# Attention units of 512 queries instead of 256 in a float32 decoder trunk

## The chip, the cores and the metric

The kernel runs on one core of one Trainium2 chip, in one launch. The metric is device time in microseconds (us); lower is better. The engines are named as in the profile: PE is the matrix engine, PEld its weight loads, DVE the vector engine, ACT the scalar engine, POOL the GpSimd engine, SP the engine that only issues DMAs. PE writes its products into PSUM, which holds 8 banks of 512 float32 per partition; four tiles `ps0` to `ps3` of two banks each cover it.

## The reference

One batch of 1024 tokens of width 1024 goes through two layers. The first layer mixes tokens with a gated linear recurrence (RG-LRU), the second with attention over 16 heads of width 64, with a forget gate; each is followed by a SwiGLU feed-forward of width 2816. All is float32. The change touches the attention of the second layer alone:

```python
for blk in range(S // Q_BLOCK):                 # 8 blocks of 128 queries
    q0, q1 = blk * Q_BLOCK, (blk + 1) * Q_BLOCK
    s = einsum('bhqd,bhkd->bhqk', q[:, :, q0:q1], k[:, :, :q1]) * HEAD_DIM ** -0.5
    s = s + c[:, :, q0:q1, None] - c[:, :, None, :q1]   # c: running sum of log forget gates
    s = where(mask, s, -inf)                    # causal
    p = softmax(s, axis=-1)
    outs.append(einsum('bhqk,bhkd->bhqd', p, v[:, :, :q1]))
```

## The kernel before, in words

Every float32 product is built from parts: an operand is split into a high part (float32r, ACT writes it) and a low part (the rest, DVE subtracts it), and PE multiplies high by high, high by low and low by high. The recurrent layer and its feed-forward take the first 990 us, the attention runs from about 1004 to 1494 us, and its output product and the second feed-forward fill the rest.

The attention goes through 8 pairs of heads, `pair(i, uses, with_p)`. Each of PE, ACT and DVE runs its own version of that function, and all three walk through the same list of steps (`pair_steps`), each doing its share of a step and skipping steps in which it has none. So the list sets the program order of all three engines at once. Each engine executes its instructions in that order; an instruction that waits for a semaphore holds back all that stand behind it on its engine. Before the change a pair has 8 units: 2 heads times 4 ranges of 256 queries, in the order 3, 0, 2, 1 (`RANGE_ORDER`). The steps are:

- `S0`, `S1`: the scores of one block of 128 queries of the **next** unit against all its keys. PE multiplies (`scores`), DVE applies the causal mask and finds the row's maximum in place in PSUM (one long instruction and a short one that reads the accumulator), ACT writes the exponentials to `probs` (`exponentials`), again with a short accumulator read, and then the tile is free ("drained"). Score tiles alternate between `ps0` and `ps1`.
- `T0`, `T1`, ...: PE transposes blocks of 128x128 exponentials of this unit into one bank of `ps2` (the two banks take turns), ACT copies the bank to `pth` (high part), DVE subtracts to `ptl` (low part). The first T of a unit waits for the exponentials of the unit's last blocks; every T waits for the `ptl` of the T two before.
- `V0`, `V1`, ...: PE multiplies the values `vs` of a block of keys by `pth` and `ptl` of the T of that number and adds up in `o_ps`, a part of `ps3`. It waits for that `ptl`.
- `O`: the finished unit is taken out of `o_ps`: ACT copies 64 partitions to `o_low`, DVE adds them to the other 64 and writes `resid`. V0 of the next unit waits for it.
- `p`: one eighth of a half of the next pair's K and Q projection, three matmuls of 512 columns. These depend on nothing of this pair, and fill PE while ACT and DVE work. Every eighth p, DVE takes the half out of PSUM. The last pair has 28 parts of the output projection in their place.
- `A`, `B` at the start: the two halves of the V projection, 24 matmuls each; `X` turns the result by 8 transposes, ACT copies it (high part of `vs`, two instructions) and `Y` is DVE's two subtractions (low part). V0 of unit 0 waits for Y. `R` turns the row sums.

Tables hang further ACT and DVE work of 1024 columns on named steps: `HI_AT` and `LO_AT` the split of the next weights, `HIGH_O_AT` and `LOW_O_AT` (last pair) the split of the attention output. After V0 of the last unit ACT also runs `high_k`, four copies of the next pair's K (lines 2119 and 2124). `tiles.plan` and `Turns` count the uses of each PSUM tile, so that waits can name them.

The lines that matter below: PE L1440 projection, L1452 and L1453 scores, L1472 transposes, L1485 values, L1518 X; ACT L2162 exponentials, L2187 and L2188 X, L2197 the copy to `pth`, L2202 `o_low`; DVE L3100 the V projection's drain, L3105 and L3106 Y, L3114 mask and maximum, L3121 `ptl`, L3130 O.

Of the kernel before, what the change touches and what calls it, by code (L numbers as in the profile page):

```python
# [11 lines left out]
P = 128  # L12
# [37 lines left out]
class FeedForward:  # L50
# [8 lines left out]
    def first_part(self, n, half):  # L59
# [10 lines left out]
RANGE_ORDER = [3, 0, 2, 1]  # L70
UNIT_STEPS = [
# [19 lines left out]
]  # L91
PAIR_START = "A S0 S1 B"
FIRST_START = "A B S0 S1"
# [11 lines left out]
FIRST_LO_AT = {(-1, "B"): "K", (3, "V0"): "Q", (6, "T2"): "nextV"}  # L105
# [7 lines left out]
def pair_steps(with_p, first):  # L113

    steps = [(-1, s) for s in (FIRST_START if first else PAIR_START).split()]
    units = UNIT_STEPS if with_p else LAST_UNIT_STEPS
    for u, unit in enumerate([FIRST_UNIT] + units[1:] if first else units):
        steps += [(u, s) for s in unit.split()]
    steps.append((len(UNIT_STEPS), "O"))
    return steps  # L120


def hawk_fox_yoco(nc, x, norm_mix, norm_ffn, w_ffn_in, w_ffn_out, w_rec_in, conv_w, conv_b,
# [21 lines left out]
    RANGES = QB // 2  # L145
# [25 lines left out]
    tiles.plan("att", [1, 0, 1] + [0, 1] * (UNITS - 1) + [0], PAIRS).plan("attE", [1, 2, 0, 1, 2, 0, 1, 2, 2])  # L171
# [25 lines left out]
    with ExitStack() as life:  # L197
# [85 lines left out]
        with ExitStack() as att:  # L283
# [17 lines left out]
            probs = [sb(f"probs{b}", [P, 2, S // (b + 1)], F32, att) for b in range(2)]  # L301
# [4 lines left out]
            o_low = [sb(f"o_low{b}", [HD, 2 * P], F32, att) for b in range(2)]  # L306
# [48 lines left out]
        o_ps = ps[3][:, 0:2 * P]  # L355
# [545 lines left out]
        def _(pool):  # L901
# [38 lines left out]
            def pool_pair(i, uses, next_k=None):  # L940
                pool.wait_ge(ql_ready, i * 2 + 2)
                pool.wait_ge(o_added, i * UNITS + 1)
# [3 lines left out]
                pool.wait_ge(o_added, i * UNITS + 4)  # L946
# [86 lines left out]
        def _(pe):  # L1033
# [422 lines left out]
            def blocks_of(r, m):  # L1456

                if m < r:
                    return [(2 * m, 0, 0), (2 * m + 1, 0, 2 * P)]
                return [(2 * m, 0, 0), (2 * m + 1, 1, 2 * P)]  # L1460

            def transposes(i, u, m):
                t = tiles_before(u) + m
                if m == 0:
                    for half in range(2):
                        slot, n = s_tile(i, u, half)
                        pe.wait_ge(drained[slot], n)
                if t >= 2 or not (isinstance(i, int) and i == 0):
                    pe.wait_ge(ptl_ready, i * T_PAIR + (t - 1))
                for kb, q0, col in blocks_of(range_of(u), m):  # L1470
                    for q in range(q0, 2):
                        last = pe.transpose(t_ps[t % 2][:, col + (q - q0) * P:col + (q - q0 + 1) * P],  # L1472
                                            probs[u % 2][:, q, kb * P:(kb + 1) * P], ident[:, :])
                last.then_inc(t_filled, 1)

            def values(i, u, m):
# [19 lines left out]
            def pair(i, uses, with_p=True):  # L1496
# [3 lines left out]
                for u, step in pair_steps(with_p, is_first(i)):  # L1500
                    m = int(step[1]) if len(step) > 1 else 0
                    if step in "AB":
                        half = "AB".index(step)
# [4 lines left out]
                        elif is_first(i):  # L1508
                            pe.wait_ge(f_drained, 2)
                        for k in range(KT):  # L1510
                            projection_part(f_bank(step), uses["V"], half, k, v_filled)
                        f += 1
                        f_read = f_before(i) + f
# [1735 lines left out]
```

## Time and profile before

| | |
|---|---|
| time, median of 3 runs | 2226.4 us (2226.28 to 2227.3) |
| span of the profiled execution, first to last instruction | 2225.0 us |
| PE busy | 2200.1 us, 99% of the span |
| DVE busy | 1674.3 us, 75% |
| ACT busy | 1181.8 us, 53% |
| POOL busy | 360.3 us, 16% |
| one pair of heads, from the same step to the same step | 60.65 us |

The profiled execution shows its span alone; what lies around it is taken as the 1.4 us that the median is longer. PE's matmuls are pipelined: a row's duration (0.39 us for 512 columns) runs into the next one's, and the time that an instruction costs PE is the distance from its start to the next start (0.23 us). The same holds in smaller measure for ACT and DVE. A short wait of PE can hide in that overlap.

### The profile page before, as it was taken

The numbers are of one execution on the slowest core, as the hardware profiler recorded it, in microseconds if no ns is written. First come the engines' busy times: TensorE is split into PE (matmuls) and PEld (weight loads), VectorE is DVE, ScalarE is ACT, GpSimd is POOL, SyncE is SP. The second block draws the span as 40 slices with busy tenths as digits, with TensorE's granted clock in tenths as the row PEclk, the third lists the DMA queues.
The fourth block names the chain that finished last, engine by engine and source line by source line (L and its number), as shares of the span: only waits on it lengthen the run. The fifth ranks groups of instructions, "written<-read, shape, count | busy, mean of one in ns | idle before, by whom it ended". The sixth has DMA issues, their size and how long they took to land.

```text
span 2225.0 us, 28679 instructions
## 1 busy us (share of the span) xinstructions
PE 2200.1 (99%) x10393; PEld 1832.6 (82%) x10393; DVE 1674.3 (75%) x2353; ACT 1181.8 (53%) x1873; POOL 360.3 (16%) x352
## 2 busy tenths in 40 slices
PE   8999999999999999999999999999999999999998
PEld 7888887888888888887888888888888888888886
DVE  7677788787778777688666766775777778888866
ACT  5543576355555555356666666754535555555525
POOL 4000000022222222021111111102002222222200
PEclk9999999999999999999999999999999999999999
DMA  5120300367676676431111111132136666666652
GB/s 152 48 59 26 95 15 24 133 133 133 132 133 133 127 131 124 129 115 29 39 30 39 39 39 39 30 105 76 39 133 117 126 124 128 127 129 128 129 168 86
DMA packets 208983, 208.03 MB, mean 93 GB/s; under 512 B 9704, under 2 KB 153296, under 8 KB 208848
## 3 DMA queue, kind: packets, MB, share of 16 engines
q0 software_dynamic: 39168, 75.51, 20.7%
q1 hardware_dynamic: 167952, 126.43, 19.1%
q10 hardware_dynamic: 1728, 4.31, 0.7%
q8 instruction: 81, 1.33, 0.2%
q14 instruction: 54, 0.44, 0.1%
HBM read 122.28 MB, written 83.95 MB: 93 GB/s over the span
## 4 chain that ended last, share of the span: by engine, by line
PE 93%; DVE 4%; ACT 1%; issue 1%; DMA 0%; ACTq 0%; POOL 0%; DVEq 0%; POOLq 0%
PE ps L1239 37%; PE ps L1044 18%; PE ps L1327 14%; PE ps L1440 10%; PE ps L1485 3%; PE ps L1472 3%; PE ps L1576 3%; PE ps L1453 1%; PE ps L1452 1%; PE ps L1555 1%; PE ps L1129 0%; PE ps L1518 0%; PE ps L1093 0%; PE ps L1412 0%; PE ps L1395 0%
## 5 line engine op out<-in xcount | busy, mean ns | idle before, releaser
L972 POOL DMA_DIRECT2D spill<-c x256 | 223.6, 926 | 727.1 <-DVE c L2698 498.4
L2567 DVE TENSOR_TENSOR ring_l<-raw_ffn,ring_h 128x512 fp32r<-128x512 f32 x320 | 222.4, 697 | 154.6 <-ACT ring_h L1804 153.2
L1804 ACT ACTIVATE ring_h<-raw_ffn 128x512 fp32r<-128x512 f32 x320 | 198.8, 625 | 196.5 <-PE ps L1239 103.7
L1897 ACT ACTIVATE c<-ps 128x512 f32<-128x512 f32 x256 | 150.2, 597 | 13.2
L1440 PE MATMUL ps<-xh,wh_att 128*128 128x512 f32 x368 | 148.6, 404 | 1.6 <-DVE wl_att L2269 1.6
L2162 ACT ACTIVATE probs<-ps,nmax 128x896 f32<-128x896 f32 (+7 forms) x128 | 95.1, 743 | 99.0 <-DVE nmax L3114 97.2
L1804 ACT ACTIVATE ring_h<-w_sum 128x512 fp32r<-128x512 f32 x112 | 69.5, 624 | 147.2 <-PE ps L1044 38.9
L1440 PE MATMUL ps<-xh,wl_att 128*128 128x512 f32 x368 | 143.9, 391 | 0.0
L1440 PE MATMUL ps<-xl,wh_att 128*128 128x512 f32 x368 | 143.9, 391 | 0.0
L3121 DVE TENSOR_TENSOR ptl<-ps,pth 128x512 fp32r<-128x512 f32 (+1 forms) x160 | 96.8, 634 | 51.8 <-ACT pth L2197 50.5
L2698 DVE TENSOR_TENSOR c<-ps,c 128x512 f32<-128x512 f32 x192 | 123.4, 683 | 4.8 <-PE ps L1327 4.5
L2306 DVE TENSOR_TENSOR resid<-ps,resid 128x1024 f32<-128x1024 f32 x76 | 92.3, 1220 | 39.3 <-PE ps L1044 31.6
L2197 ACT ACTIVATE pth<-ps 128x512 fp32r<-128x512 f32 (+1 forms) x160 | 82.8, 553 | 35.0 <-PE ps L1472 25.0
L1327 PE MATMUL ps<-hl,ring_h 128*128 128x512 f32 x256 | 99.8, 390 | 0.0
L1327 PE MATMUL ps<-hh,ring_h 128*128 128x512 f32 x256 | 99.7, 390 | 0.0
L1327 PE MATMUL ps<-hh,ring_l 128*128 128x512 f32 x256 | 99.6, 389 | 0.0
L3114 DVE CUSTOM_DVE_ANT_0 ps<-ps,causal 128x896 f32<-128x896 f32 (+7 forms) x128 | 94.5, 774 | 0.0
L2567 DVE TENSOR_TENSOR ring_l<-w_sum,ring_h 128x512 fp32r<-128x512 f32 x112 | 76.5, 684 | 22.0 <-ACT ring_h L1804 22.0
L1472 PE MATMUL ps<-ident,probs 128*128 128x128 f32 x576 | 81.5, 275 | 2.1 <-DVE ptl L3121 1.2
L1440 PEld LDWEIGHTS ps<-xh,wl_att 128*128 128x128 f32 x368 | 69.1, 188 | 15.6
L1485 PE MATMUL ps<-pth,vs 128*128 128x256 f32 x320 | 80.6, 279 | 0.7 <-DVE ptl L3121 0.4
L1440 PEld LDWEIGHTS ps<-xh,wh_att 128*128 128x128 f32 x368 | 69.3, 188 | 12.8 <-issue 2.0
(411 smaller groups left out, 6305.5 us busy)
## 6 DMA issues: line engine op xcount, KB each, us to landing
spill<-c POOLq DMA_DIRECT2D x256, 256.0 KB, 5.9
raw_ffn<-in_w_ffn_in SPq DMA_DIRECT2D x88, 512.0 KB, 5.3
raw_ffn<-in_w_ffn_out SPq DMA_DIRECT2D x44, 512.0 KB, 7.3
resid<-spill SPq DMA_DIRECT2D x24, 512.0 KB, 7.2
raw<-in_w_rec_in SPq DMA_DIRECT2D x16, 512.0 KB, 5.6
spill<-resid POOLq DMA_DIRECT2D x16, 512.0 KB, 3.0
raw_att<-in_w_kvf SPq DMA_DIRECT2D x16, 512.0 KB, 4.0
xin<-in_x SPq DMA_DIRECT2D x4, 1024.0 KB, 9.8
```

Source lines behind the costliest of these rows:

```text
L972: pool.dma_start(spill[m, :, half * BANK:(half + 1) * BANK], block[:, :], accum_op=ALU.add).then_inc(sem, 16)
L1044: last = pe.matmul(acc[:, h], w, v[:, h], start=(first and p == 0), stop=(final and p == 2))
L1239: last = pe.matmul(acc, w, v, start=(start and k == 0 and p == 0), stop=(k == 3 and p == 2), skip_group_check=True)
L1327: last = pe.matmul(acc, a, v, start=(i in (P1, P2, P5) and p == 0), stop=(p == 2), skip_group_check=True)
L1440: last = pe.matmul(acc, w, v[:, k, h], start=(k == 0 and p == 0), stop=(k == KT - 1 and p == 2))
L1472: last = pe.transpose(t_ps[t % 2][:, col + (q - q0) * P:col + (q - q0 + 1) * P], probs[u % 2][:, q, kb * P:(kb + 1) * P], ident[:, :])
L1485: last = pe.matmul(o_ps[:, q0 * P:2 * P], v, pt[t % 2][:, col:col + n], start=(kb == 0 and pt is pth), stop=(kb == 2 * r + 1 and pt is ptl))
L1804: act.activation(F.ring_h[slot][:, :], src, ACT.Copy).then_inc(F.unit_hi, 1)
L1897: act.activation(dst[:, :], y if what == "s5" else w, ACT.Copy).then_inc(out_tapped, 1)
L2567: dve.tensor_tensor(F.ring_l[slot][:, :], src, F.ring_h[slot][:, :].bitcast(F32), ALU.subtract).then_inc(F.unit_lo, 1)
L2698: dve.tensor_tensor(c, w if what == "C22" else y, c, ALU.add).then_inc(out_joined, 1)
L3121: dve.tensor_tensor(ptl[t % 2][:, 0:width], t_ps[t % 2][:, 0:width], pth[t % 2][:, 0:width].bitcast(F32), ALU.subtract).then_inc(ptl_ready, 1)
```

## The change

A unit now is one head and 512 queries, so a pair has 4 units: for each head first the wide range (queries 512 to 1023, against up to 1024 keys), then the narrow one (queries 0 to 511). Each unit has four score blocks S0 to S3 of the next unit. A T tile holds one block of keys against up to four blocks of queries, in place of two blocks of keys against two blocks of queries; the last three key blocks of the diagonal are packed as 384 + 128 and 256 columns. A wide unit has 7 T tiles and a narrow one 3, so a pair has 20 as before. The V matmuls have up to 512 columns, `o_ps` grows from 256 to 512 columns, and `o_low` with it. The V projection is cut as A, B, C, with B and C four eighths each of the second half. The score tiles keep alternating between `ps0` and `ps1`. All step strings and the tables that hang work on steps are new.

```diff
-RANGE_ORDER = [3, 0, 2, 1]
+RANGE_ORDER = [1, 0]
 UNIT_STEPS = [
-    "T0 T1 X p p Y S0 T2 T3 p V0 V1 S1 p p V2 V3",
-    "O T0 S0 S1 p V0 p p",
...
-    "O T0 T1 R p p p p V0 V1",
+    "T0 X T1 p p p Y V0 T2 p V1 T3 S0 p V2 T4 S1 p V3 T5 S2 p V4 T6 S3 p V5 V6",
+    "O T0 T1 S0 S1 p p V0 T2 p p S2 S3 V1 p p V2 p p",
+    "O T0 T1 p p V0 T2 p V1 T3 S0 p V2 T4 S1 p V3 T5 S2 p V4 T6 S3 p V5 p V6",
+    "O T0 T1 p p V0 T2 R p p V1 p p V2 p p",
 ]
+FIRST_UNIT = "p X Y p T0 T1 p p V0 T2 p V1 T3 S0 p V2 T4 S1 p V3 T5 S2 p V4 T6 S3 p V5 V6"
+FIRST_THIRD = "O T0 T1 p V0 T2 p V1 T3 S0 p V2 T4 S1 p V3 T5 S2 p V4 T6 S3 p V5 V6"
+FIRST_FOURTH = "O T0 T1 p p V0 T2 R p V1 p V2 p p"
 LAST_UNIT_STEPS = [
+    "T0 X T1 Y V0 T2 p V1 T3 S0 p V2 T4 S1 V3 T5 S2 p V4 T6 S3 p V5 V6",
+    "O T0 T1 S0 S1 p p V0 T2 p p S2 S3 V1 p p V2 p p",
...
-PAIR_START = "A S0 S1 B"
-FIRST_START = "A B S0 S1"
+PAIR_START = "A S0 S1 B S2 S3 C"
+FIRST_START = "A B C S0 S1 p p p S2 S3"
...
-HI_AT = {(-1, "A"): "K", (3, "T1"): "Q", (4, "V2"): "nextV"}
-LO_AT = {(-1, "S1"): "K", (3, "V0"): "Q", (6, "T2"): "nextV"}
+HI_AT = {(-1, "A"): "K", (1, "V0"): "Q", (2, "V2"): "nextV"}
+LO_AT = {(-1, "S1"): "K", (1, "V1"): "Q", (3, "T2"): "nextV"}
...
-            o_low = [sb(f"o_low{b}", [HD, 2 * P], F32, att) for b in range(2)]
+            o_low = [sb(f"o_low{b}", [HD, BANK], F32, att) for b in range(2)]
...
-        o_ps = ps[3][:, 0:2 * P]
+        o_ps = ps[3][:, 0:BANK]
...
             def blocks_of(r, m):
-                if m < r:
-                    return [(2 * m, 0, 0), (2 * m + 1, 0, 2 * P)]
-                return [(2 * m, 0, 0), (2 * m + 1, 1, 2 * P)]
+                if m <= 4 * r:
+                    return [(m, 0, 0)]
+                if m == 4 * r + 1:
+                    return [(m, 1, 0), (m + 2, 3, 3 * P)]
+                return [(m, 2, 0)]
...
             def transposes(i, u, m):
                 if m == 0:
-                    for half in range(2):
-                        slot, n = s_tile(i, u, half)
-                        pe.wait_ge(drained[slot], n)
+                    for n in range(2, 4):
+                        slot, count = s_tile(i, u, n)
+                        pe.wait_ge(drained[slot], count)
```

ACT's program in the first unit of a pair, before (a pair in the loop, from X to the unit's end; `pth<-ps` is the copy of a T, `probs` the exponentials of an S, `vs` is X):

```order
L2187 ACTIVATE vs<-ps 128x8x64
L2188 ACTIVATE vs<-ps 128x8x64
L2162 ACTIVATE probs,rsum<-ps,nmax 128x128
L2197 ACTIVATE pth<-ps 128x512
L2197 ACTIVATE pth<-ps 128x384
L2162 ACTIVATE probs,rsum<-ps,nmax 128x256
L2202 ACTIVATE o_low<-ps 64x256
```

The same place in the changed kernel:

```order
L2171 ACTIVATE probs,rsum<-ps,nmax 128x1024
L2206 ACTIVATE pth<-ps 128x512
L2196 ACTIVATE vs<-ps 128x8x64
L2197 ACTIVATE vs<-ps 128x8x64
L2206 ACTIVATE pth<-ps 128x512 x3
L2171 ACTIVATE probs,rsum<-ps,nmax 128x128
L2206 ACTIVATE pth<-ps 128x512
L2171 ACTIVATE probs,rsum<-ps,nmax 128x256
L2206 ACTIVATE pth<-ps 128x512
L2171 ACTIVATE probs,rsum<-ps,nmax 128x384
L2206 ACTIVATE pth<-ps 128x256
L2171 ACTIVATE probs,rsum<-ps,nmax 128x512
```

Before, two copies and two exponentials follow X; now the copy of T1 stands behind X, and four exponentials alternate with copies, one each, down to the unit's end.

ACT's program at the end of a pair, before (`kh` are the four copies of `high_k`, `o_low` the step O):

```order
L2202 ACTIVATE o_low<-ps 64x256
L2197 ACTIVATE pth<-ps 128x512
L2197 ACTIVATE pth<-ps 128x384
L2119 ACTIVATE kh<-kv_tmp 64x1024 x2
L2124 ACTIVATE kh<-kh 64x1024 x2
L2219 DMA rinv_dram<-rinv_rows 16x128
L2202 ACTIVATE o_low<-ps 64x256
```

And in the changed kernel:

```order
L2211 ACTIVATE o_low<-ps 64x512
L2206 ACTIVATE pth<-ps 128x512 x2
L2128 ACTIVATE kh<-kv_tmp 64x1024 x2
L2133 ACTIVATE kh<-kh 64x1024 x2
L2206 ACTIVATE pth<-ps 128x256
L2228 DMA rinv_dram<-rinv_rows 16x128
L2211 ACTIVATE o_low<-ps 64x512
```

The four copies of K stood behind the last T of the pair; now the copy of the last T, T2, stands behind them.

## Rows read from the trace of the kernel before

**Rows 1.** The page's busy shares, and the engines of its chain.
```profile
PE 2200.1 (99%) x10393; PEld 1832.6 (82%) x10393; DVE 1674.3 (75%) x2353; ACT 1181.8 (53%) x1873; POOL 360.3 (16%) x352
PE 93%; DVE 4%; ACT 1%; issue 1%; DMA 0%; ACTq 0%; POOL 0%; DVEq 0%; POOLq 0%
```

**Rows 2.** One pair of heads in the view by stretches, with its columns.
```profile
core 0: us, PE busy (x) PEld busy (x) DVE busy (x) ACT busy (x) POOL busy (x), PEclk, DMA share, GB/s
1258.47:1319.13 60.66, 60.58 (x355) 52.54 (x354) 41.38 (x77) 38.55 (x73) 10.12 (x6) 1.00 0.13 36
```

**Rows 3.** Timeline of PE, unit 0 and 1 (start, duration, instruction, count).
```profile
1264.86 1.06 PE L1518 MATMUL ps<-ident,kv_tmp 128*128 128x128 f32 x8
1265.68 0.48 PE L1440 MATMUL ps<-xh,wh_att 128*128 128x512 f32 x1
1266.00 0.39 PE L1440 MATMUL ps<-xl,wh_att 128*128 128x512 f32 x1
1266.23 0.40 PE L1440 MATMUL ps<-xh,wl_att 128*128 128x512 f32 x1
...
1268.83 0.28 PE L1485 MATMUL ps<-pth,vs 128*128 128x256 f32 x1
1268.94 0.28 PE L1485 MATMUL ps<-ptl,vs 128*128 128x256 f32 x1
...
1272.11 0.22 PE L1485 MATMUL ps<-pth,vs 128*128 128x128 f32 x1
1272.17 0.28 PE L1485 MATMUL ps<-ptl,vs 128*128 128x128 f32 x1
1272.44 0.52 PE L1472 MATMUL ps<-ident,probs 128*128 128x128 f32 x3
```

**Rows 4.** Timeline of DVE, units 0 and 2; in brackets idle time and its releaser.
```profile
1264.02 0.69 DVE L3100 TENSOR_TENSOR kv_tmp<-ps,rstd 128x512 f32<-128x512 f32 x1 [1.79 <-PE ps L1440]
...
1267.69 0.68 DVE L3106 TENSOR_TENSOR vs<-ps,vs 128x512 fp32r<-128x512 f32 x1
1268.29 0.29 DVE L3114 CUSTOM_DVE_ANT_0 ps<-ps,causal 128x128 f32<-128x128 f32 x1
...
1270.18 1.15 DVE L3121 TENSOR_TENSOR ptl<-ps,pth 128x512 fp32r<-128x512 f32 x2 [1.55 <-ACT pth L2197]
1271.26 0.42 DVE L3114 CUSTOM_DVE_ANT_0 ps<-ps,causal 128x256 f32<-128x256 f32 x1
...
1279.42 0.56 DVE L3114 CUSTOM_DVE_ANT_0 ps<-ps,causal 128x384 f32<-128x384 f32 x1
...
1279.89 0.73 DVE L3114 CUSTOM_DVE_ANT_0 ps<-ps,causal 128x512 f32<-128x512 f32 x1
1280.54 0.14 DVE L3114 DVE_READ_ACCUMULATOR2_ANT nmax<- 128x1 f32 x1
```

**Rows 5.** Timeline of ACT, the same stretches, and the end of the pair.
```profile
1266.45 0.59 ACT L2188 ACTIVATE vs<-ps 128x512 fp32r<-128x512 f32 x1
1268.67 0.37 ACT L2162 ACTIVATE probs<-ps,nmax 128x128 f32<-128x128 f32 x1 [1.62 <-DVE nmax L3114]
...
1269.55 0.98 ACT L2197 ACTIVATE pth<-ps 128x512 fp32r<-128x512 f32 x2 [0.43 <-PE ps L1485]
1271.77 0.47 ACT L2162 ACTIVATE probs<-ps,nmax 128x256 f32<-128x256 f32 x1 [1.24 <-DVE nmax L3114]
...
1280.06 0.58 ACT L2162 ACTIVATE probs<-ps,nmax 128x384 f32<-128x384 f32 x1 [1.40 <-DVE nmax L3114]
...
1280.71 0.69 ACT L2162 ACTIVATE probs<-ps,nmax 128x512 f32<-128x512 f32 x1
...
1281.39 0.48 ACT L2197 ACTIVATE pth<-ps 128x384 fp32r<-128x384 f32 x1
...
1308.70 2.12 ACT L2119 ACTIVATE kh<-kv_tmp 64x1024 fp32r<-64x1024 f32 x2
```

**Rows 6.** The last 5 us of the span in the view by stretches, columns as in rows 2.
```profile
2220.00:2225.00 5.00, 0.00 (x0) 0.00 (x0) 2.11 (x4) 0.53 (x3) 0.00 (x0) 0.51 0.57 219
```

More of the change, by code:

```diff
@@ L116, in pair_steps @@
     units = UNIT_STEPS if with_p else LAST_UNIT_STEPS
-    for u, unit in enumerate([FIRST_UNIT] + units[1:] if first else units):
+    for u, unit in enumerate([FIRST_UNIT, units[1], FIRST_THIRD, FIRST_FOURTH] if first else units):
         steps += [(u, s) for s in unit.split()]
@@ L184, in hawk_fox_yoco @@
     SUMMED = {seg: n * RUN_SUMS for seg, n in STAT.items()}
-    T_PAIR = RANGES * (RANGES + 1)
-    OUT_HI_AT = {(-1, "A"): 0, (0, "Y"): 1, (UNITS - 2, "T2"): 2}
-    OUT_LO_AT = {(-1, "S1"): 0, (1, "S1"): 1, (UNITS - 2, "V2"): 2}
+    T_PAIR = 2 * sum(4 * r + 3 for r in range(RANGES))
+    OUT_HI_AT = {(-1, "A"): 0, (0, "Y"): 1, (UNITS - 2, "V4"): 2}
+    OUT_LO_AT = {(-1, "S1"): 0, (0, "T4"): 1, (UNITS - 1, "T1"): 2}
     O_SPLITS = PAIRS
@@ L300, in hawk_fox_yoco @@
             vs = sb("vs", [P, 2, QB, 2, HD], F32R, att)
-            probs = [sb(f"probs{b}", [P, 2, S // (b + 1)], F32, att) for b in range(2)]
+            probs = [sb(f"probs{b}", [P, n], F32, att) for b, n in enumerate((26 * P, 10 * P))]
             pth = [sb(f"pth{b}", [P, BANK], F32R, att) for b in range(2)]
@@ L723, in range_of, with s_tile, wide_of, probs_of @@
             return RANGE_ORDER[u % RANGES]
-        def s_tile(i, u, half):
-            return tiles.use("att", half if u == 0 else 2 * u + half + 1, i)
+        def s_tile(i, u, n):
+            return tiles.use("att", n if u == 0 else 4 * u + n + 1, i)
         def vt_tile(i):
-            return tiles.use("att", 2, i)
+            return tiles.use("att", 4, i)
         def rsum_tile(i):
-            return tiles.use("att", 2 * UNITS + 1, i)
+            return tiles.use("att", 4 * UNITS + 1, i)
+        def wide_of(u, n):
+            return (4 * range_of(u) + n + 1) * P
+        def probs_of(u, n):
+            first = sum(wide_of(u, q) for q in range(n))
+            return probs[u % 2][:, first:first + wide_of(u, n)]
         def f_before(i):
@@ L1482, in values @@
                     v = vs[:, j, kb, :, :].rearrange("p a d -> p (a d)")
-                    n = (2 - q0) * P
+                    n = (4 - q0) * P
                     for pt in (pth, ptl):
-                        last = pe.matmul(o_ps[:, q0 * P:2 * P], v, pt[t % 2][:, col:col + n],
-                                         start=(kb == 0 and pt is pth), stop=(kb == 2 * r + 1 and pt is ptl))
-                last.then_inc(o_filled if m == r else pt_used, 1)
+                        last = pe.matmul(o_ps[:, q0 * P:BANK], v, pt[t % 2][:, col:col + n],
+                                         start=(kb == 0 and pt is pth), stop=(kb == 4 * r + 2 and pt is ptl))
+                last.then_inc(o_filled if m == 4 * r + 2 else pt_used, 1)
             def head_ready(i, j):
@@ L1507, in pair @@
                                 pe.wait_ge(forget_dve, INVERSE_USED)
-                        elif is_first(i):
+                        elif step == "A" and is_first(i):
                             pe.wait_ge(f_drained, 2)
[L1510 to L1513, printed above, removed]
+                        for k in {"A": range(KT), "B": range(KT // 2), "C": range(KT // 2, KT)}[step]:
+                            projection_part(f_bank("AB"[half]), uses["V"], half, k, v_filled)
+                        if step != "B":
+                            f += 1
+                            f_read = f_before(i) + f
                     elif step == "X":
```

76 lines of the change are left out of this document (38 added, 38 removed), and 15 rows, old and new, of tables (LAST_UNIT_STEPS, UNIT_STEPS).

## The prediction

> **What bounds the kernel now.** I read the page first: PE is busy for 99% of the span and makes up 93% of the chain that ended last [rows 1]. Next the view by stretches for one pair of heads: PE is busy 60.58 us of 60.66, DVE 41.4, ACT 38.6, at the full clock [rows 2]. So PE's program sets the time here, and ACT and DVE are hidden, each with a third of its time free. Last the timelines of PE, DVE and ACT through a pair, to get the distance from one start to the next, which is what an instruction costs [rows 3 to 5]. The list of steps is what keeps ACT and DVE hidden: after each T it puts enough p and V in front of PE. The change rewrites that list, so two sums are needed: PE's work, and whether ACT and DVE still keep ahead of it.
>
> **PE's own work.** Scores, projections and transposes keep their counts and columns. The V matmuls of a pair were 64 of 256 columns and 16 of 128. Now they are 24 of 512, 8 of 384, 8 of 256 and 8 of 128, with the same sum of columns. A 512-column matmul costs 0.23 us, one of 256 costs 0.11 to 0.12, a couple of 128-column ones about 0.17 (1266.00 to 1266.23, 1268.83 to 1268.94, and 1272.11 to 1272.17 with as much again as a 256-column one) [rows 3]. Merging thus gives under 0.01 us each, and the four fewer short couples 0.05 us each: 0.3 us less per pair. Against it, the first matmul behind a run of transposes costs 0.32 instead of 0.23 us (1265.68 to 1266.00) [rows 3], and a pair has 16 such runs instead of 13: 0.3 us more. PE's work is the same to 0.1 us. Whatever happens comes from waits.
>
> **The round trip in a wide unit.** "T3 S0 p V2 T4 S1 p V3 T5 S2 p V4 T6 S3 p V5 V6" has four rounds in which ACT copies a T, DVE subtracts it, DVE masks an S, and ACT takes its exponentials before it may copy the next T. Each of the four stands behind the one before it, on its own engine or by its data. Its time, from starts in the rows:
> - ACT's copy of 512 columns to DVE's subtraction: 0.63 us (1269.55 to 1270.18).
> - DVE's subtraction to its S: 0.61 us for 512 columns (two of 512 and 384 take 1.08, 1270.18 to 1271.26, of which the 384 is 0.47).
> - DVE's S to ACT's exponentials: 0.38 us for 128 columns, 0.51 for 256, 0.64 for 384 (1268.29 to 1268.67, 1271.26 to 1271.77, 1279.42 to 1280.06). For 512: 0.65 to DVE's accumulator read plus the 0.17 that the hand-over took at 384, 0.82.
> - Exponentials to ACT's next instruction: 0.39 us for 128, 0.52 for 256, 0.65 for 384, 0.70 for 512 (1280.06 to 1280.71 to 1281.39; for the narrower two the duration and the accumulator read, less their overlap).
>
> So the rounds take 2.01, 2.27, 2.53 us, and the last, whose T6 has only 256 columns (copy to subtraction 0.42, subtraction 0.34), 2.28: together 9.1 us [rows 4, 5]. It starts when ACT sees T3, 0.37 us for four transposes (eight take 0.82, 1264.86 to 1265.68) plus 0.26 for the hand-over from PE (X's transposes end their turn at 1265.68, and ACT began the first of its two copies 0.49 before 1266.45, at 1265.96) [rows 3, 5]. The next unit's T0 needs the last exponentials: 0.63 + 9.1 + 0.1 = 9.8 us after T3's start. PE's work in between: T3 to T6 1.3, S0 to S3 1.2 plus 0.09 four times after transposes, four p 2.8, V2 to V4 1.4, V5 0.53, V6 0.24, in sum 7.8. PE waits 2.0 us, first at V6 (its ptl comes at 8.3, PE is there at 7.6), then at T0. Before, no S stood in such an alternation for more than two rounds, and the narrow S went with p on both sides.
>
> In unit 2 the same run also carries the split of the next V weights at V2: ACT loses 1.0 us, PE has one p (0.7) more. Wait 2.2 to 2.3 us.
>
> **The other waits of a pair.**
> - V0 of unit 0 needs Y. Before, ACT ran T0, T1, X and DVE Y behind them, with p p S0 T2 T3 p on PE as cover. Now ACT copies T1 behind X, and DVE subtracts T1 before Y. From X's end: ACT starts X at 0.26, ends it at 1.35 (two of 0.49 and 0.59), copies T1 (0.49 until free, 0.63 until DVE can start), DVE T1 at 1.98, Y from 2.6 to 3.9, V0 at 4.0. PE has T1 and three p, 2.55 us. Wait 1.45 us [rows 4, 5].
> - X needs C's drain: 0.26 + 0.69 + 0.1 = 1.05 us after C (the drain's duration at 1264.02) [rows 4]. T0 alone covers 0.37, where T0 and T1 covered 0.74. Wait 0.7 us, before 0.3.
> - V2 of unit 3: T2's copy stands behind the four copies of K, 4.3 us at 1.07 each (two take 2.12) [rows 5]. From T0's start: T1's copy ends at 1.6, the K copies at 5.9, T2's ptl at 6.8. PE's work until there, with six p, is 6.35. Wait 0.5 us. Nothing stood behind these copies before but O.
> - K's second half is taken out of PSUM behind S3 and a weight split on DVE: 0.3 us at the next p.
> - O: 512 columns instead of 256, half as often. Bounds for one: from the old 0.38 on ACT to the 0.59 of a full-width copy of 512 columns [rows 5]; I take the upper one on ACT and 0.69 on DVE. Two p cover it. Nothing.
>
> Sum for a pair: 2.0 + 2.2 + 1.45 + 0.7 + 0.5 + 0.3 = 7.1 us. The same reckoning on the old list finds 0.7 us (the narrowest: T0 of unit 1 at 1272.44, 0.2 us after its turn [rows 3]), and a pair of 59.9 us against the measured 60.65; so it is good to about 1 us a pair, and if anything low. Net 6.4 us, times the six pairs in the loop 38.4 us.
>
> **First and last pair.** In the first, the third unit has no p at V5 and two fewer p in all, and the last unit has one p instead of two before V1 and before V2, so the wait behind the K copies grows to 1.9 us; in all 10.7 us of waits against 3.5 before, +7 us. In the last pair the same gaps of ACT and DVE must also hold the splits of the attention output, twice eight operations of 0.6 to 1.1 us, and V0 follows T1 without any p: that wait alone becomes about 4 us, T0 before it 2, the rounds of unit 0 4.9 instead of 2.0. I get 19 us against 3.4, +15.5. This last term is the least certain; its lower bound is a pair like the others, 6.4.
>
> **Total.** 38.4 + 7 + 15.5 = 61 us. The profiled span 2225.0 plus 61 plus the 1.4 us around it gives 2287 us; the median of the runs stands 1.4 above the span, so it is 61 above the median of 2226.4 too. Bounds: hand-overs between engines of 0 or 0.08 us in place of 0.04 give 55 and 66, the lower end of the last pair takes 9 off, and rounds that are a tenth shorter (0.9 us in each of 16 wide units) would take 15 off. Together 2256 to 2305.
>
> **The clock.** In this trace the granted clock stays at the full 2.4 GHz (1.00) through the pair and falls to about the 1.2 GHz level (0.51) only in the last 5 us, when PE had no instruction at all [rows 2, 6]. The waits that I predict are 0.3 to 1.5 us long with dense work between, so I leave the clock alone. The Trainium skill, page "TensorE: Matmul & The Clock Gate", section "A second HAM failure mode: psum-queue depth-cycling", says that frequent short idle moments between groups of matmuls can make the clock swing between its two levels. By that rule the changed kernel would lose more than its waits. The rival for it is worked out below from rows.
>
> **Rivals.**
> 1. The V savings win and the rounds stay hidden. For it: ACT and DVE are only two thirds busy per pair, and fewer, longer matmuls and half as many O. It needs a round of ACT and DVE to fit in PE's 1.8 to 2.0 us per T, so it decides at whether DVE's mask of an S really waits behind ptl, and ACT's next copy behind the exponentials. Then the old waits (0.7) and 0.3 us of matmul work go, eight times: 2226 - 8 = 2218 us. Against it: ACT was idle for 1.24 to 1.62 us on nmax before exponentials [rows 5] with this same order; the chain is there, it just was short.
> 2. Half of it: the alternation costs nothing, since the queue ahead of it gives more lead than I grant, but Y, X and the K copies cost. 1.45 + 0.4 + 0.5 = 2.35 us in seven pairs and 6 in the last: 2226 + 22 = 2249 us.
> 3. The clock falls after the waits. If after each of the two longest waits of a pair one run of 24 matmuls' worth (5.4 us at 0.23 each) went at half speed, that is 10.9 more per pair: 61 + 87, 2374 us.
> 4. The waits turn out hidden and the savings too, no change: 2226 us.
>
> **How the numbers follow.** Forecast 0.77, rival 1 0.05, rival 2 0.11, rival 3 0.03, rival 4 0.04. A difference under 0.2%, 4.5 us, can't be told from none by this measurement. Slower is the forecast with rivals 2 and 3, 0.91; same 0.04; faster 0.05. The range 2256 to 2305 leaves out rivals 1, 3 and 4 and most of 2.
>
> **What would show it.** In the changed profile a pair in the loop should take about 67 us, with PE busy below 95% of it and the clock at 1.00. PE's idle time should be charged at the values line to ptl (V6) and to the subtraction of Y (V0), and at the transposes line to the exponentials (T0 of units 1 and 3), 2 us per wide unit. ACT should run copy, exponentials, copy without a pause other than for DVE, and its copy of T2 in the last unit should come right behind the four K copies. The matmul starts within V should stand 0.23 us apart. I am wrong if the pair stays at 60 to 61 us, or if PE waits mostly elsewhere, as at O.

## The result, and the profile after

The changed kernel takes 2289.6 us (median of 4 runs, 2288.2 to 2294.2), the kernel before 2226.6 us beside it. The ratio is 1.0286, with a 95% interval of 1.0273 to 1.0299: slower by 63 us, where 61 were forecast. The profiled execution has a span of 2286.4 us and a mean granted clock of 0.995.

The page's busy shares, its chain by engines, and the groups that answer for the new idle time (busy us, mean ns, then idle time in front of the group and what ended it):

```profile
PE 2216.1 (97%) x10137; PEld 1820.6 (80%) x10137; DVE 1671.5 (73%) x2321; ACT 1174.7 (51%) x1841; POOL 360.2 (16%) x352
PE 84%; DVE 7%; ACT 5%; issue 3%; DMA 0%; ACTq 0%; DVEq 0%
L3130 DVE TENSOR_TENSOR ptl<-ps,pth 128x512 fp32r<-128x512 f32 (+1 forms) x160 | 99.8, 636 | 156.8 <-ACT pth L2206 155.8
L2171 ACT ACTIVATE probs<-ps,nmax 128x640 f32<-128x640 f32 (+7 forms) x128 | 94.9, 741 | 133.7 <-DVE nmax L3123 132.3
L1480 PE MATMUL ps<-ident,probs 128*128 128x128 f32 x576 | 88.2, 280 | 19.0 <-issue 16.3
```

DVE and ACT do the same work as before in a longer span [rows 1], but are now in the chain with 12% instead of 5%. The two wait for each other: DVE at `ptl` for ACT's copy, ACT at the exponentials for DVE's maximum.

PE's waits, whole program (engine and line that waited, for whom: total us, times, longest us):

```profile
PE ps L1480 <- issue: 16.3, 16, 1.0
PE ps L1493 <- DVE ptl L3130: 12.0, 20, 1.5
PE ps L1493 <- DVE vs L3115: 9.2, 7, 2.7
PE ps L1136 <- DMA xin<-in_x: 7.0, 1, 7.0
PE ps L1447 <- DVE wl_att L2278: 4.1, 2, 2.2
```

L1493 is the values line, L1480 the transposes. Two waits in each of the eight pairs carry the label "issue". They are T0's waits of units 1 and 3: the line begins just after ACT's last exponentials of the unit before. The fourth row is the kernel's first load, as before. The fifth is in the first pair only: a wait of 2.0 us, where the kernel before waits 1.6, and one of 2.2 that is new.

Stretches, columns as in rows 2: 2 us of the first pair, 66 us of the loop, and the start of the last pair.

```profile
1042.00:1044.00 2.00, 2.00 (x9) 1.81 (x8) 1.77 (x4) 1.08 (x2) 0.00 (x0) 0.50 0.00 0
1200.00:1266.00 66.00, 61.54 (x321) 49.98 (x320) 40.55 (x72) 37.58 (x69) 10.09 (x6) 1.00 0.12 33
1490.00:1500.00 10.00, 5.18 (x28) 4.01 (x27) 7.36 (x11) 6.77 (x11) 0.00 (x0) 0.78 0.00 0
1500.00:1510.00 10.00, 10.00 (x43) 8.35 (x43) 4.79 (x8) 2.25 (x5) 0.00 (x0) 0.70 0.01 2
```

PE is busy for 93% of the loop, where it was busy for all of it [rows 2]. The clock is 1.00 there, in every 2 us of all six loop pairs. It falls three times: from 1041 to 1045 us in the first pair, and from 1495 to 1506 and from 1516 to 1520 us in the last.

The chain, start of B in two pairs that follow each other (start, us, what), which gives the length of a pair:

```profile
1219.30 2.75 PE ps L1447 x12
...
1285.73 2.75 PE ps L1447 x12
```

A pair is 66.43 us, also as a mean over five; before it was 60.65. PE's rows with idle time in unit 0 (start, duration, in brackets the idle time and its releaser):

```profile
1227.66 1.07 PE L1527 MATMUL ps<-ident,kv_tmp 128*128 128x128 f32 x8 [0.22 <-DVE kv_tmp L3109]
...
1232.32 0.50 PE L1493 MATMUL ps<-pth,vs 128*128 128x512 f32 x1 [1.07 <-DVE vs L3115]
...
1234.48 0.60 PE L1480 MATMUL ps<-ident,probs 128*128 128x128 f32 x4
...
1242.64 0.38 PE L1493 MATMUL ps<-pth,vs 128*128 128x256 f32 x1 [0.51 <-DVE ptl L3130]
1242.86 0.28 PE L1493 MATMUL ps<-ptl,vs 128*128 128x256 f32 x1
1244.16 1.06 PE L1480 MATMUL ps<-ident,probs 128*128 128x128 f32 x8 [1.02 <-issue]
```

These are X, V0, T3, V6 and the next unit's T0. And ACT's side of the same unit:

```profile
1235.12 0.60 ACT L2206 ACTIVATE pth<-ps 128x512 fp32r<-128x512 f32 x1 [0.99 <-PE ps L1480]
1236.74 0.37 ACT L2171 ACTIVATE probs<-ps,nmax 128x128 f32<-128x128 f32 x1 [1.02 <-DVE nmax L3123]
...
1237.10 0.59 ACT L2206 ACTIVATE pth<-ps 128x512 fp32r<-128x512 f32 x1
1238.84 0.47 ACT L2171 ACTIVATE probs<-ps,nmax 128x256 f32<-128x256 f32 x1 [1.16 <-DVE nmax L3123]
...
1239.31 0.59 ACT L2206 ACTIVATE pth<-ps 128x512 fp32r<-128x512 f32 x1
1241.18 0.58 ACT L2171 ACTIVATE probs<-ps,nmax 128x384 f32<-128x384 f32 x1 [1.29 <-DVE nmax L3123]
...
1241.75 0.37 ACT L2206 ACTIVATE pth<-ps 128x256 fp32r<-128x256 f32 x1
1243.28 0.69 ACT L2171 ACTIVATE probs<-ps,nmax 128x512 f32<-128x512 f32 x1 [1.16 <-DVE nmax L3123]
...
1244.08 0.59 ACT L2211 ACTIVATE o_low<-ps 64x512 f32<-64x512 f32 x1
```

Copy, exponentials, copy, four times without a break but for DVE's answer. From copy to copy the rounds take 1.98, 2.21, 2.44 and 2.33 us; 2.01, 2.27, 2.53 and 2.28 were reckoned. From T3 to the next T0, PE needs 9.68 us, reckoned 9.8. ACT has 4.6 us of idle time in this stretch, all of it waits for DVE: an engine with four tenths of its time free in the loop (37.58 us busy of 66) that is late nonetheless.

By stages, from the starts of each pair's A in the chain (the last pair ends with the attention): the first pair grew from 65.0 to 75.5 us, each of the six loop pairs from 60.65 to 66.43, the last from 60.6 to 78.0. That is 10.5 + 34.7 + 17.4 = 62.6 us. The profiled spans differ by 61.4, so nothing was lost behind the attention; about 1 us came back there.

### The profile page after: what moved, and what is told of

It is laid out like the page before. It is cut to its first block, busy times and chain, and to the rows that moved or that the text cites. A ratio compares the mean times of both kernels' runs of the same rounds, so it can differ in the third digit from the quotient of the medians.

```text
span 2286.4 us, 27989 instructions
## 1 busy us (share of the span) xinstructions
PE 2216.1 (97%) x10137; PEld 1820.6 (80%) x10137; DVE 1671.5 (73%) x2321; ACT 1174.7 (51%) x1841; POOL 360.2 (16%) x352
## 4 chain that ended last, share of the span: by engine, by line
PE 84%; DVE 7%; ACT 5%; issue 3%; DMA 0%; ACTq 0%; DVEq 0%
PE ps L1246 36%; PE ps L1051 17%; PE ps L1334 13%; PE ps L1447 6%; PE ps L1585 3%; DVE ptl L3130 2%; PE ps L1493 2%; PE ps L1480 2%; ACT pth L2206 2%; DVE ps L3123 1%; PE ps L1458 1%; PE ps L1459 1%; ACT kh L2128 1%; ACT probs L2171 1%; PE ps L1136 0%
## 5 line engine op out<-in xcount | busy, mean ns | idle before, releaser
L2171 ACT ACTIVATE probs<-ps,nmax 128x640 f32<-128x640 f32 (+7 forms) x128 | 94.9, 741 | 133.7 <-DVE nmax L3123 132.3
L1480 PE MATMUL ps<-ident,probs 128*128 128x128 f32 x576 | 88.2, 280 | 19.0 <-issue 16.3
L1480 PEld LDWEIGHTS ps<-ident,probs 128*128 128x128 f32 x576 | 71.3, 144 | 39.0 <-issue 22.5
L3123 DVE CUSTOM_DVE_ANT_0 ps<-ps,causal 128x640 f32<-128x640 f32 (+7 forms) x128 | 95.9, 766 | 4.5 <-PE ps L1459 3.9
L1493 PE MATMUL ps<-pth,vs 128*128 128x512 f32 x192 | 69.0, 359 | 21.7 <-DVE ptl L3130 12.0
```

## The experiments

Theory: the time is the sum of the waits that the new order makes, each removable by moving its steps. Rivals: the merged V matmuls or the clock are what costs, or the waits stand in for each other, so that removing one only shows the next. In what follows a pair's length is a mean over the loop's pairs, read from the chain as above.

**1. Y ahead of T1 in unit 0 (`y_first`).**

```
-    "T0 X T1 p p p Y V0 T2 ...
+    "T0 X Y T1 p p p V0 T2 ...
```

> The changed kernel with Y ahead of T1 in the six pairs of the loop: on DVE the two subtractions of Y stand before the subtraction of T1; PE's and ACT's programs stay as they are. My theory: V0 of unit 0 waits for Y, which stands behind T1 on DVE, so the wait at V0 (1.07 us seen as idle in a pair of the changed trace) shrinks by about 1.2 us a pair, with nothing lost elsewhere: 6 x 1.2 = 7 us less than the changed kernel, about 2282 us. Rival: the wait is set by ACT's copies of X and the transposes ahead of them, and DVE's order doesn't matter: no change, 2289 to 2290 us.

Measured: 2285.2 us (2282.1 to 2285.3), ratio 1.0258 [1.0241, 1.0275]; a pair of 65.34 us, 1.09 less. The wait of V0 on Y is left in the last pair only, whose list was not edited. PE's waits:

```profile
PE ps L1493 <- DVE vs L3115: 2.7, 1, 2.7
```

The wait was real and nothing took its place in the loop. It was worth 1.1 us, not 1.45. The median fell by 4.5 us and not by the 6.5 of six loop pairs: in the profile B of the second pair starts 2.1 us later than in the changed kernel, though no list ahead of it was edited, and in the first pair the clock fell twice (1020 to 1024 and 1044 to 1048 us) instead of once.

**2. The K copies behind T2 of unit 3 (`k_late`).**

```
-                    if with_p and (u, step) == (UNITS - 1, "V0"):
+                    if with_p and (u, step) == (UNITS - 1, "T2"):
```

> The changed kernel with the four copies of the next pair's K hung on T2 of the last unit instead of V0, so that on ACT they stand behind T2's copy. My theory: V2 of the last unit waited for T2's copy behind them, 0.5 us in each of the six loop pairs and about 1.9 us in the first: 4 to 5 us less than the changed kernel, 2285 us. Rival: the copies only delay the next pair's start by as much as they free V2: no change, 2289 to 2290 us.

Measured: 2283.5 us (2283.3 to 2286.5), ratio 1.0259 [1.0242, 1.0276]; a pair of 65.80, 0.63 less. In the first pair V2 had waited 1.50 us (1077.75 in the changed kernel's trace), and C of the second pair starts 1.4 us earlier here. With six loop pairs that makes 5.2 of the 6.1 us between the medians, so the rival falls.

**3. S in couples in the wide units (`s_couples`).**

```
-    ... V1 T3 S0 p V2 T4 S1 p V3 T5 S2 p V4 T6 S3 p V5 V6   (units 0 and 2)
+    ... V1 T3 p V2 T4 S0 S1 p V3 T5 p V4 T6 S2 S3 p V5 V6
```

> The changed kernel with the narrow scores of the wide units in the loop put in couples: 'T3 p V2 T4 S0 S1 p V3 T5 p V4 T6 S2 S3' in place of one S behind each of T3 to T6. Same instructions. My theory: the waits in the wide units come from the round trip ACT copy, DVE subtraction, DVE mask, ACT exponentials, and halving the number of rounds that hold an S shortens them: a loop pair 3.4 us shorter, 20 us less than the changed kernel, about 2270 us. Rival 1: the waits come from T and V of 512 columns themselves (ptl arrives late whatever the S do): no change, 2289 us. Rival 2: S2 and S3 now stand last, so T0 of the next unit waits as much longer as the rounds are shorter: within 3 us of the changed kernel.

Measured: 2271.0 us (2268.2 to 2272.0), ratio 1.0195 [1.0178, 1.0212]; a pair of 63.37, 3.06 less. PE's waits:

```profile
PE ps L1480 <- issue: 8.1, 10, 1.0
PE ps L1493 <- DVE ptl L3130: 6.3, 8, 1.5
```

The waits on exponentials and `ptl` fall by half. The steps and their number are the same, only two S stand together instead of one behind each T. So the alternation of T and S is what made the rounds serial.

**4. The V matmuls cut back to at most 256 columns (`v_256`).**

```
-                    for pt in (pth, ptl):
-                        last = pe.matmul(o_ps[:, q0 * P:BANK], ...
+                    cuts = [(0, n)] if n <= 2 * P else [(0, 2 * P), (2 * P, n)]
+                    for a, b in cuts:
+                        for pt in (pth, ptl):
+                            last = pe.matmul(o_ps[:, q0 * P + a:q0 * P + b], ...
```

> The changed kernel with every V matmul of more than 256 columns cut in pieces of at most 256, as many columns and weight loads per column as before the change; orders, tiles and waits stay. My theory: wide V matmuls are worth almost nothing on PE, 0.3 us a pair and partly behind waits: 1 to 3 us more than the changed kernel, 2290 to 2293 us. Rival: wide V matmuls are worth much and the new orders lost still more (a load of weights costs PE 0.1 us or more each, 32 more of them in a pair): 25 us or more above, 2315 us.

Measured: 2292.4 us (2291.4 to 2292.9), ratio 1.0294 [1.0277, 1.0311]; a pair of 66.60, 0.17 more. The merge is not what costs; it brings 0.2 us a pair here, where part of it lies in waits. The two medians are 2.7 us apart and the runs of the two kernels overlap; what is refuted is the rival's 25 us.

**5. Edits 1, 2 and 3 together (`three_edits`).**

```
-    "T0 X T1 p p p Y V0 T2 p V1 T3 S0 p V2 T4 S1 p ...
+    "T0 X Y T1 p p p V0 T2 p V1 T3 p V2 T4 S0 S1 p ...
...
+                    if with_p and (u, step) == (UNITS - 1, "T2"):
```

> The changed kernel with the three edits of y_first, k_late and s_couples together, in the loop pairs (k_late's in all pairs that have it). My theory: the three waits are separate, so the gains add up (1.1 + 0.6 + 3.1 us per loop pair by the traces of the three) or do a little better, since a shorter round also frees V6 and T0: a loop pair of 61.3 to 61.6 us, the kernel at about 2257 to 2260 us. Rival: the waits stand in one another's shadow, and the largest alone brings most: 2268 to 2271 us.

Measured: 2257.9 us (2257.1 to 2262.0), ratio 1.0139 [1.0123, 1.0154]; a pair of 61.66, which is 4.77 less. The three single gains sum to 1.09 + 0.63 + 3.06 = 4.78. The waits are separate and add up: the rival by which one stands in for the next falls.

**6. A new order for all lists (`reordered`).** Same units and same computation, wide V matmuls kept.

```
-    "T0 X T1 p p p Y V0 T2 p V1 T3 S0 p V2 T4 S1 p V3 T5 S2 p V4 T6 S3 p V5 V6",
-    "O T0 T1 S0 S1 p p V0 T2 p p S2 S3 V1 p p V2 p p",
-    "O T0 T1 p p V0 T2 p V1 T3 S0 p V2 T4 S1 p V3 T5 S2 p V4 T6 S3 p V5 p V6",
-    "O T0 T1 p p V0 T2 R p p V1 p p V2 p p",
+    "T0 T1 X Y p S0 T2 p p V0 p T3 V1 V2 T4 S1 p V3 T5 T6 V4 p S2 S3 V5 V6 p p",
+    "O T0 T1 S0 p p S1 p T2 V0 S2 p S3 p p p V1 p V2",
+    "O T0 T1 S0 p p V0 T2 V1 p p T3 T4 V2 p S1 V3 T5 T6 V4 S2 S3 p p p V5 V6",
+    "O T0 T1 R p p p V0 T2 V1 p p p p V2 p",
...
-HI_AT = {(-1, "A"): "K", (1, "V0"): "Q", (2, "V2"): "nextV"}
+HI_AT = {(-1, "A"): "K", (1, "T1"): "Q", (2, "T4"): "nextV"}
...
+    OUT_HI_AT = {(-1, "A"): 0, (0, "T5"): 1, (UNITS - 2, "V1"): 2}
```

> The changed kernel's units, tiles and instructions with new step strings and hooks for all pairs: T in couples (T3 T4 ... T5 T6) followed by couples of V, the S of a wide unit spread or in couples, Y directly behind X, p spread over all units. My theory: nothing but the order made the changed kernel slower, so the orders can give all of it back; reckoned as in the prediction, a loop pair takes 0.6 us less than before the change, since the T couples save transitions and the V matmuls 0.3 us: 2222 us, between 2218 and 2228. Rival: units of 512 queries have waits of their own that no order hides (T0 of the narrow unit on the last exponentials, a whole unit in one PSUM bank that O must empty): 2240 us or more.

Measured: 2233.4 us (2232.2 to 2234.6, 6 runs), ratio 1.0031 [1.0019, 1.0043]; a pair of 60.06, below the 60.65 of before. The time lies above the range that was expected and below the rival's. What stands out is one wait in the last pair. PE's waits, and the queue and DVE there:

```profile
PE ps L1494 <- DVE ptl L3131: 7.2, 2, 6.7
```

```profile
1454.05 25.41 SPq L883 DMA_DIRECT2D resid<-spill  x7
1479.56 0.38 SPq L780 DMA_DIRECT2D kv_tmp<-in_w_o  x1
```

```profile
1478.42 0.69 DVE L3095 TENSOR_TENSOR xl<-resid,xh 128x512 fp32r<-128x512 f32 x1
1487.36 1.29 DVE L3131 TENSOR_TENSOR ptl<-ps,pth 128x512 fp32r<-128x512 f32 x2 [8.25 <-ACT pth L2207]
```

I had moved the split of the third output weight to V1 of unit 2. Its load stands in SP's program behind seven reloads of `resid`, and SP waits before each of them until DVE has split a further piece of the attention output (`sp.wait_ge(ol_ready, 4 + k // 2 + 1)` in the kernel). They went out as DVE came to these splits, the last at 1479.14, behind the `xl` of 1478.42, and the load of the weight at 1479.56. ACT stood at the split, the copies of T behind it, and DVE and PE behind those.

**7. The kernel before, with its K copies early (`before_k_early`).** The same hook of `high_k`, in the old order, at T0 of its unit 7: the copy of T1 then stands behind the copies of K.

```
-                    if with_p and (u, step) == (UNITS - 1, "V0"):
+                    if with_p and (u, step) == (UNITS - 1, "T0"):
```

> The kernel before the change with the four copies of the next pair's K hung on T0 of its last unit instead of V0, so that on ACT they stand ahead of T1's copy. It puts into the kernel before the one wait that I hold the change for having brought at the end of a pair. My theory: V1 of the last unit waits 2.5 us in each of the seven pairs: 2226.7 + 17.8 = 2244 us. Rival: PE's lead in the last unit or a shorter start of the next pair takes it in: 2227 to 2230 us.

Measured: 2252.1 us (2251.5 to 2252.7), ratio 1.0113 [1.0098, 1.0129]; a pair of 64.69, 4.04 more. I had expected 2244. The wait on `ptl` comes once a pair and takes up to 2.2 us, and PE is slow behind it:

```profile
1263.07 0.39 PE L1485 MATMUL ps<-pth,vs 128*128 128x256 f32 x1 [2.17 <-DVE ptl L3121]
...
1264.41 0.63 PE L1440 MATMUL ps<-xh,wl_att 128*128 128x512 f32 x1
1264.84 0.63 PE L1440 MATMUL ps<-xh,wh_att 128*128 128x512 f32 x1
...
1267.28 0.40 PE L1440 MATMUL ps<-xh,wh_att 128*128 128x512 f32 x1
1267.52 0.40 PE L1440 MATMUL ps<-xl,wh_att 128*128 128x512 f32 x1
```

```profile
1262.00:1264.00 2.00, 0.93 (x6) 0.83 (x7) 1.54 (x3) 0.43 (x2) 0.00 (x0) 0.93 0.00 0
1264.00:1268.00 4.00, 4.00 (x13) 3.15 (x12) 3.60 (x5) 3.64 (x5) 0.00 (x0) 0.61 0.30 90
1268.00:1271.00 3.00, 3.00 (x15) 2.47 (x14) 2.12 (x2) 1.81 (x2) 0.00 (x0) 1.00 0.20 57
```

Starts are 0.43 us apart for some eight matmuls, then 0.24 again, and the granted clock is 0.61 in that stretch: the 1.2 GHz level for most of it. The run of 24 matmuls takes 7.1 us. Behind the first pair the same run takes 5.5: PE waited just as long before it (2.17 us, until 1070.61), and the clock stayed at 1.00. Of the 4.0 us, then, about 2.4 are wait and 1.6 clock. The wait was forecast rightly, and the clock, which I had left out, came on top in the six pairs behind the first.

**8. Reordered, with new first and last pairs (`reordered2`).** The loop is that of experiment 6.

```
+FIRST_SECOND = "O p T0 T1 p S0 S1 V0 p p T2 S2 S3 p p V1 p V2 p"
+FIRST_THIRD = "O T0 T1 p S0 S1 V0 V1 T2 T3 p S2 S3 T4 V2 p p T5 V3 V4 T6 p V5 V6"
...
-    "T0 X T1 Y V0 T2 p V1 T3 S0 p V2 T4 S1 V3 T5 S2 p V4 T6 S3 p V5 V6",
+    "X p S0 Y T0 T1 p p S1 S2 V0 T2 V1 T3 p p S3 V2 V3 T4 T5 p p V4 T6 V5 V6",
...
-    "O T0 T1 p p V0 T2 p R p V1 p p V2 p p p",
+    "O T0 T1 p p V0 T2 R p V1 V2",
...
-    OUT_HI_AT = {(-1, "A"): 0, (0, "Y"): 1, (UNITS - 2, "V4"): 2}
+    OUT_HI_AT = {(-1, "A"): 0, (0, "T5"): 1, (UNITS - 2, "V6"): 2}
```

> The reordered kernel with a new order for the first and the last pair; the loop pairs keep theirs (60.07 us measured, 60.65 before the change). In the last pair the split of the third output weight stands after V6 of the third unit instead of V1, so that ACT doesn't stand still for a DMA that lands late. My theory: that one wait (6.7 us seen) was what kept the reordered kernel above the kernel before; without it the units of 512 queries are as fast as the old ones or a little faster: 2222 us, between 2219 and 2226. Rival: the last pair has no room for its extra splits in units of 512 queries, and another wait takes the place: 2230 us or more.

Measured: 2227.2 us (2224.9 to 2228.7, 11 runs) beside 2226.8 for before (21 runs), ratio 1.0001 [0.9992, 1.0010]; a pair of 60.03. PE's longest waits on DVE:

```profile
PE ps L1448 <- DVE wl_att L2279: 2.0, 1, 2.0
PE ps L1494 <- DVE ptl L3131: 1.7, 3, 0.9
```

With order alone the whole loss is given back. The time can't be told from the kernel before, and it lies 1 us above the range of 2219 to 2226 that was expected: in the profile the six loop pairs are 3.7 us shorter than before the change, but the first and the last pair about 1 us longer each. The load of the third output weight goes out as late as in experiment 6 (1479.37); ACT now asks for it later.

**9. Reordered2 with V cut to 256 columns (`reordered2_256`),** the edit of experiment 4.

```
+                    cuts = [(0, n)] if n <= 2 * P else [(0, 2 * P), (2 * P, n)]
```

> reordered2 with every V matmul of more than 256 columns cut in pieces of at most 256, in the same order. Here PE hardly waits, so the difference to reordered2 is what wide V matmuls are worth by themselves. My theory: 0.3 us a pair, 2 to 3 us in all: 2224.5 us. Rival 1: each extra weight load costs PE 0.1 us: 25 us more. Rival 2: nothing at all, since PE takes 256-column matmuls at exactly half the time: the same as reordered2.

Measured: 2229.2 us (2228.6 to 2231.3, 11 runs), ratio 1.0012 [1.0003, 1.0021]; a pair of 60.60. With the waits gone, the merge of the V matmuls is worth 0.57 us a pair and 2 us in the medians, 0.1%, as forecast; both its rivals fall. That is all that the wide matmuls bring.

**10. The changed kernel with the last pair of reordered2 (`last_reordered`).** The last pair's lists and hooks of experiment 8, the rest as changed.

```
-    "T0 X T1 Y V0 T2 p V1 T3 S0 p V2 T4 S1 V3 T5 S2 p V4 T6 S3 p V5 V6",
+    "X p S0 Y T0 T1 p p S1 S2 V0 T2 V1 T3 p p S3 V2 V3 T4 T5 p p V4 T6 V5 V6",
```

> The changed kernel with the order of reordered2 in its last pair alone. My theory: the 17.4 us that the last pair took longer than before the change (78.0 against 60.6, the granted clock falling to 0.70 to 0.83 in three stretches of 10 us) are waits of its order and the slow matmuls that follow them, nothing that comes from the pairs ahead: the last pair takes 60 to 62 us, the kernel 2272 to 2274 us. Rival: the clock falls there for another reason (the load on ACT, DVE and DMA at the end of the attention), so that a good part of the loss stays: 2278 us or more.

Measured: 2276.2 us (2272.5 to 2277.1), ratio 1.0216 [1.0200, 1.0232]. The same stretches as above, which now have another clock:

```profile
1490.00:1500.00 10.00, 8.59 (x48) 6.83 (x47) 8.95 (x14) 6.35 (x13) 0.00 (x0) 1.00 0.07 18
1500.00:1510.00 10.00, 9.55 (x51) 7.29 (x50) 8.66 (x17) 7.13 (x17) 0.00 (x0) 1.00 0.28 107
```

From its first matmul of A (1481.46) to the first one behind the attention (1543.64) the last pair takes 62.2 us instead of 78, much as expected. So it gave back 16 of its 17.4 us, the clock's share among them. The profiled span is only 11.2 us shorter than the changed kernel's, because the first pair lost 3.3 us more (B of the second pair at 1089.78 against 1086.46) and the rest behind the attention 1.4. In the first pair PE waits for the low part of the Q weights. The row of this kernel, then two of the changed one at the same place:

```profile
1053.72 0.76 PE L1447 MATMUL ps<-xh,wh_att 128*128 128x512 f32 x1 [2.94 <-DVE wl_att L2278]
```

```profile
1053.10 0.47 PE L1447 MATMUL ps<-xh,wh_att 128*128 128x512 f32 x1 [2.16 <-DVE wl_att L2278]
1053.41 0.40 PE L1447 MATMUL ps<-xl,wh_att 128*128 128x512 f32 x1
```

That wait is 2.2 us in the changed kernel's profile and 2.9 here. Behind it the clock stayed at 1.00 there, and here 14 matmuls were slow (5.7 us to the next T, 3.1 there). The two profiles also differ ahead of it: here the clock fell at 1019 us, there at 1041. This first pair is the same program in both, so where the clock falls in it changes from one execution to the next. The 3.3 us are of the size by which the runs of one kernel with this first pair differ (3 to 6 us from lowest to highest in most), but with one profile for each kernel it isn't shown to be the reason.

## Why the prediction was right

The time of 2287 us and the range hold. By its own steps:

- **PE's work.** Reckoned at no change, with 0.3 us gained by the merge and 0.3 lost at transitions. The merge measured 0.17 us a pair behind waits and 0.57 without them (experiments 4, 9). V's starts are 0.23 us apart, as forecast. Right in sign, small either way.
- **Wide units.** 2.0 us for unit 0, first at V6, then at T0. From the rows above, with each instruction charged up to where the next one could start, V6 waits 0.67 (behind a couple of 128 columns that began at 1241.80 and takes 0.17) and T0 1.18 (behind V6's second, 1242.86 and 0.12): 1.85 us. Putting the S in couples took 3.06 of the 4.2 us of both units. This is the largest term, and its mechanism is shown.
- **V0 behind Y.** 1.45 forecast, 1.09 measured. In the changed kernel V0 starts 1.47 us behind the start of the last p matmul, which costs 0.23: a wait of 1.24. In experiment 1 it starts 0.38 behind it and still only 0.06 behind the end of Y, so 0.15 of the wait is left there, hidden in the overlap of rows. Against 1.45 the chain of ACT and DVE was reckoned 0.25 us too long (3.75 us from T1's start to V0, where 4.0 were reckoned), most of it in X's two copies, whose overlap was not taken off.
- **K copies.** 0.5 forecast for V2 of unit 3; 0.63 measured, with all that moving them changes. V2 itself shows no idle time: it starts 0.49 us behind the last p matmul instead of 0.23, and its two matmuls are 0.22 apart instead of 0.11, so 0.37 are lost there.
- **X behind C's drain.** 0.4 net forecast. The profile shows 0.22 of idle time at X; from start to start T0 comes 0.26 late and X another 0.48, 0.7 in all, as reckoned before the 0.3 of the old kernel was taken off. No run took this term alone. With it, the steps of K's second half, and the waits that the couples leave, the last 1.6 us between 61.66 and 60.03 were removed together by the new order and are not told apart.
- **O.** Nothing was forecast, and O shows no wait.
- **Loop pair.** 6.4 forecast, 5.78 measured: 38.4 against 34.7 us. Terms a little too large, above all Y.
- **First pair.** 7 forecast, 10.5 measured. Here the reckoning missed a wait: the first pair's 17th p, in unit 1, needs the low part of the Q weights, which is split only at V1. That is the 2.2 us of `wl_att`. Another 1.3 us at a p, on `q_tmp`, was missed too, and so was 1.6 us of clock (below). Together that is more than the 3.5 that are missing, so the waits that were reckoned are about 1.6 us too large.
- **Last pair.** 15.5 forecast, 17.4 measured. The order's waits are right in kind: 2.1 us at T0 and 2.7 at V0, where 2 and 4 were forecast. Some 4.4 us of the 17.4 are clock, for which nothing was forecast.
- **The range.** The lower end follows from its terms (61 - 6 - 9 - 15, 2257 us). The upper one does not: the terms given end at 66, which is 2292 us; 2305 needs rounds that are a tenth longer as well.
- **The clock.** Left alone in the forecast. True for the six loop pairs, whose waits of 0.2 to 1.1 us leave it at 1.00. Not true in the first pair, where it fell behind waits of 0.63 and 1.02 us, and not in the last: 0.78 and 0.70 around the last three of these rows of PE.

```profile
1041.21 1.49 PE L1480 MATMUL ps<-ident,probs 128*128 128x128 f32 x8 [1.02 <-issue]
1042.36 0.78 PE L1458 MATMUL ps<-kl,q 128*128 128x512 f32 x1
...
1494.60 0.63 PE L1480 MATMUL ps<-ident,probs 128*128 128x128 f32 x4 [2.09 <-ACT probs L2171]
1495.06 1.32 PE L1527 MATMUL ps<-ident,kv_tmp 128*128 128x128 f32 x8
...
1499.97 0.80 PE L1493 MATMUL ps<-pth,vs 128*128 128x512 f32 x1 [2.73 <-DVE vs L3115]
```

So rival 3 did happen, in two pairs of eight. X's eight transposes took 1.32 us there and 1.07 in the loop. What it cost can be estimated from the same steps at both levels. From T0's start to the p behind the two scores PE needs 3.86 us in the first pair and 3.75 in the last (1516.51 to 1520.26), and 2.30 in the first pair of `last_reordered`, where the clock stayed up at that place. From V0 to the third matmul of the p behind T3 and S0 it needs 6.06 us in the last pair and 3.29 in the loop. With 0.2 for X that is 1.6 us in the first pair and 4.4 in the last, some 6 of the 61 us that the profiled spans differ by. The Trainium skill, page "TensorE: Matmul & The Clock Gate", section "A second HAM failure mode: psum-queue depth-cycling", puts a clock that swings between its two levels down to frequent short pauses between groups of matmuls. The trace agrees with it at most in part: in the loop, with six such pauses of 0.2 to 1.1 us a pair, the clock never fell, while in the first and the last pair it did, once in each behind the same 1.02 us of T0. Why 61 us came out so close is thus partly luck: the loop was 3.7 us over, the two ends 5.4 under, and the two ends hold the 6 us of clock for which the sum has no term. Without them the loss is about 57 us.

Rivals 1, 2 and 4 fall by the measured time. Rival 1's saving exists, but at 2 us and only with another order (experiment 9).

## What to carry to other kernels

An order list that several in-order engines share has to be timed by round trips, not by each engine's load: ACT and DVE had a third of their time free and still made PE wait, because each copy of a T stood behind the exponentials of the S before it. Put two T's or two S's together, so that each engine has its next input while the other answers, put long copies behind the last short one that somebody waits for, and go over the first and last rounds apart, since they have less work for cover. A wider matmul of the same number of columns is not worth an order that waits: here it brought 0.6 us a pair, and the order cost 5.8.

## What was not expected of the hardware

- The length of a wait did not tell whether PE's clock would fall. Behind one of 2.17 us (`before_k_early`, 1263.07) some eight matmuls ran at the 1.2 GHz level, 0.43 us apart, and cost 1.6 us more; behind one of 2.17 in the same kernel (1070.61) and one of 2.16 in the changed kernel (1053.10) the clock stayed at 1.00. Behind the 1.02 us of T0 it fell in the changed kernel's first pair and stayed at 1.00 in all six loop pairs. What sorts these cases no run here shows.
- A DMA can be late for a wait that isn't its own. The load of a weight went out at 1479.56, though what it writes over was free since X's transposes (1446.35): it stood in SP's program behind reloads that waited for DVE's splits, the last of them at 1478.42. When ACT asked for it too early, 6.7 us of that showed on PE.
